# Splitting the down weights in two stages, starting the second up group with the last chunk, and three buffers for its results

## The chip, the cores and the metric

The kernel runs on one core of one Trainium2 chip. The metric is the device time of one execution in microseconds. Its engines are the tensor engine (PE, with its weight loads PEld), VectorE (DVE), ScalarE (ACT), GpSimd (POOL) and SyncE (SP), which here only issues DMAs.

## The reference, cut to what matters

One layer of a hybrid decoder over 2048 prompt rows and 64 sample rows of width 1024, in float32: a norm, a projection into eight attention heads and four mLSTM heads, both mixers, an output projection with a residual, and an MLP.

```python
def sqrelu_mlp(h, w_up, w_down):
    u = jnp.einsum('btd,df->btf', h, w_up)
    return jnp.einsum('btf,fd->btd', jnp.square(jax.nn.relu(u)), w_down)
...
h = rms_norm(x, norm2_g)
x = x + sqrelu_mlp(h, w_up, w_down)    # d_ff = 4096
y = rms_norm(x, norm_f_g)
```

The outputs also hold the sample caches of 2048 rows each, moved up by eight rows: 96 copies of 680 KB from one DRAM tensor to another, which nothing in the layer waits for.

## The kernel before, in words

**Products.** Float32 accuracy comes from splitting each operand into a rounded high part (float32r) and the low rest: ScalarE rounds (a Copy into float32r), VectorE or GpSimd subtracts, and a product is three matmuls, high × high, high × low, low × high (lines 2639 to 2641). The MLP's products are done by a seven-product scheme over 2 × 2 blocks (Winograd's form of Strassen's), so each operand also needs four sums of its blocks: seven slots instead of four.

**Stages.** `project` (line 243) works in two groups of rows, eight tiles and nine. After eight chunks of q/k for the mLSTM, each group makes five token blocks (40 + 45 tiles): the tensor engine fills one of two banks, VectorE's `tile_out` (646) rotates and copies it into a `stage` slot (two slots in group 0, three in group 1), ScalarE's `keep` (502) issues its store. GpSimd's `lo_token` (415) makes the low part of the next block's weights in two halves of 2048 columns. SyncE issues 20 of the cache copies beside group 0 (`copies`, 349). Then come `mixers`, `project_out` and `mlp` (2651).

**Up, in `mlp`.** There are 48 sets in a written order (2672): sets 0 to 15 are chunks 0 to 15 of the up weights on the first 1024 rows (512 columns a product), sets 16 to 47 the same chunks on the other rows, in two halves q of 272 columns. A set is seven chains of 12 matmuls into four banks of one of two bank sets. ScalarE's `first` (3008) copies the first chain's bank into `made[s % 2][0]`, which the fifth chain waits for; VectorE's `up_post` (3153) adds banks into three `made` buffers; ScalarE's `squares` (2980) applies relu and square and stores the four results to `K.u` in DRAM. Because the `made` buffers are two sets deep, a buffer written again waits for the store of two sets before (`u_out`). Chunk c+1's weights are loaded when set c begins, summed by VectorE (`up_sums`), rounded by ScalarE (`w_hi`) and split by VectorE (`w_low`). The operands of chunks 0 and 1 are also stored to DRAM when made (`keep`, 2800) and loaded again for sets 16 to 19 (`load_kept`, 2805); line 2839 makes SyncE wait for those stores.

**Units.** The down weights are prepared beside Up in 32 units of 256 columns: SyncE loads a quarter (`load_unit`, 2787), VectorE makes four sums (`unit_sums`, 3177), ScalarE rounds 1792 columns (`unit_hi`, 3015), VectorE splits (`unit_low`, 3187), SyncE stores both parts to `K.wd` (`store_unit`, 2793). There is one buffer, so a unit's load waits for the landed stores of the one before. They lie in sets 0 to 14, in every even set from 18 to 44, and in 27, 33 and 39 (2675). In each of these sets VectorE's queue has the sums between `up_post(s, 2)` and `up_post(s, 3)` (3249). SyncE issues one cache copy per set besides.

**Change of group.** In set 15 SyncE loads the second group's h (1088 KB a slot, five loads, 2843 to 2853) into the slots that finished chains leave. VectorE makes the sums and low parts of half q = 0, GpSimd the sums of half q = 1 (2918 to 2926), VectorE its low parts in set 16.

**Down.** 64 steps of seven chains of six matmuls (512 columns), four steps for each of 16 passes over an eighth of d_ff, with 8 short sample steps. Per step SyncE loads u (`load_u`, 2763) and a part of the next eighth of weights (`load_down`, 2822: one DMA for the high, one for the low parts), GpSimd makes u's sums (`sums`, 2928), ScalarE rounds, VectorE splits and adds into `acc` (`down_post`, 3279). GpSimd's program has `sums(0)`, `sums(1)`, then a wait for the final norm's gain (2946), then the rest. The gain's load is issued after the first step's weights (2896).

Of the kernel before, what the change touches and what calls it, by code (L numbers as in the profile page):

```python
# [6 lines left out]
F32 = mybir.dt.float32  # L7
# [6 lines left out]
P = 128  # L14
# [228 lines left out]
def project(K):  # L243
# [8 lines left out]
    with ExitStack() as ctx:  # L252
# [17 lines left out]
        wq_raw = xb[:, 1]  # L270
        xn = sb("xn", [P, 2, D])
# [31 lines left out]
        gated, dve_own, pe_state, act_state = sem("p1_gated"), sem("p1_dve_own"), sem("p1_pe_state"), sem("p1_act_state")  # L303
        tail_zero, tail_mm, tail_ev, tail_out = sem("p1_tail_zero"), sem("p1_tail_mm"), sem("p1_tail_ev"), sem("p1_tail_out")
# [20 lines left out]
        QB = (0, 16)  # L325

# [3 lines left out]
        def _(sp):  # L330
# [23 lines left out]

            for g in range(2):
                if g == 0:
                    norm.sync_group(sp, GN[0], constants)
                else:
                    for T in range(GT0[1], GT0[1] + GN[1]):
                        norm.load(sp, T, T % 2, False)  # L360
                        if T == GT0[1] + 1:
                            sp.wait_ge(lo_ready, 13)
                            load_first()
# [9 lines left out]
                for b in range(1, 5):  # L373
                    sp.wait_ge(lo_ready, b + (base + 8))
                    sp.dma_start(w_raw[:], K.w_tok[b]).then_inc(wt_in, 16)
                    if g == 0:
                        if b > 1:
                            copies(GN[0] * (b - 2) + 3, 8 if b < 4 else 4)
# [8 lines left out]
                    if b == 3:  # L387
                        tables.sync_m(sp)
                        for s in range(3):
                            sp.wait_ge(stage_out[s], 16 * (6 + (20 if s < 2 else 0)))  # L390
# [14 lines left out]
        def _(pool):  # L405
# [14 lines left out]

            qr = wq_raw.rearrange("p (k c) -> p k c", k=KC)
            for g in range(2):
# [6 lines left out]
                if g == 0:  # L429
                    lo_token(g, 1, 1)  # L430
                    with pool.Fori(1, 2) as i:
                        for j in range(2):
                            lo_token(g, 2 * i + j, j)
# [8 lines left out]
                lo_token(g, 4, 0)  # L442

        @block.scalar
        def _(act):
# [56 lines left out]
            def keep(g, b, t, slot):  # L502
                T = GT0[g] + ORDER[g][t]
                act.wait_ge(tok_ready, 40 * g + b * GN[g] + t + 1)
# [4 lines left out]
                act.dma_start(dst[T * P:(T + 1) * P, :], stage[:, slot]).then_inc(stage_out[slot], 16)  # L509

# [14 lines left out]
            for g in range(2):  # L525
                n, nn = NPC[g], GN[g]
                if g == 0:
# [4 lines left out]
                    round_chunk(0, 1, 1)  # L532
                evac(g, 0, 0, g > 0)
# [21 lines left out]
                R = 2 if g == 0 else 3  # L555
                round_block(g, 1, (qk_mm, QB[g] + n * 8))
                for t in range(nn):
                    keep(g, 0, t, t % R)
                round_block(g, 2, (tok_mm, 40 * g + nn))
                for t in range(nn):  # L560
                    keep(g, 1, t, t % R)
# [4 lines left out]
                for t in range(nn):  # L566
                    keep(g, 2, t, t % R)
# [3 lines left out]
                for t in range(nn):  # L571
                    keep(g, 3, t, t % R)
# [4 lines left out]
                for t in range(nn):  # L577
                    keep(g, 4, t, t % R)
# [23 lines left out]
        def _(dve):  # L602
# [43 lines left out]
            def tile_out(g, b, j, t, kind):  # L646
                R = 2 if g == 0 else 3
# [3006 lines left out]
```

## Time and profile before

| what | value |
|---|---|
| median of the runs | 2994.52 us (2981.97 to 2996.72, three runs) |
| profiled execution | 2992.78 us, span 2991.0 us |
| mean granted tensor clock | 0.960 of full speed |
| busy: PE, PEld, DVE, ACT, POOL | 92%, 77%, 61%, 36%, 22% of the span |
| Up (sets 0 to 47) | about 1524.7 to 2283.3 us |
| Down | 2283.3 us to the end |
| HBM | 461.65 MB read, 244.95 MB written |

The span runs from the first to the last instruction of the profiled execution; the execution's own time is 1.8 us longer. In rows of stretches each engine has its busy time and, in brackets, its instructions in the stretch; then come the granted tensor clock as a share of full speed, the mean share of time in which the 16 DMA engines moved packets, and GB/s. Lines are those of the kernel before. A helper's line stands for all who call it. Where a set begins is read from every 84th matmul of lines 2639 to 2641.

### The profile page before, as it was taken

What the parts mean: (1) busy time and instruction counts of PE and PEld (TensorE: products, weight loads), DVE (VectorE), ACT (ScalarE), POOL (GpSimd) and SP (SyncE); (2) the same over time, 40 slices, a digit from 0 to 9 for tenths busy, and PEclk for the clock granted to TensorE, in tenths of its full rate; (3) what the DMA queues carried; (4) which work ended last, traced back from release to release, by engine and by line L of the source; (5) the groups of instructions that cost most, each with busy time, mean ns of one, the idle gap of its engine ahead of it and who ended that gap; (6) DMA issues with size and microseconds to landing.
All of it is one profiled execution on the core that took longest, in us unless ns stands there. A gap on an engine that the chain in (4) does not pass through costs nothing. (4 is left out here: it accounts for less than half of the span.)

```text
span 2991.0 us, 46001 instructions
## 1 busy us (share of the span) xinstructions
PE 2737.8 (92%) x17331; PEld 2293.8 (77%) x17331; DVE 1834.0 (61%) x3890; ACT 1079.5 (36%) x1984; POOL 651.7 (22%) x539
## 2 busy tenths in 40 slices
PE   7999999999999978999879998888887999899996
PEld 5878788778777766678767886888776888778885
DVE  5522555233788755577566666555554777877776
ACT  4301322111676752423354554544443111321113
POOL 1212012120455440211100001000001344533333
PEclk9999999999999988999989998999999999999998
DMA  4464243444464548957567779576779677776762
GB/s 155 150 233 154 95 139 130 158 131 147 129 203 134 171 157 319 407 205 262 205 229 261 271 267 336 202 251 236 241 246 337 231 248 248 258 271 224 238 234 76
DMA packets 348899, 642.33 MB, mean 215 GB/s; under 512 B 39375, under 2 KB 237139, under 8 KB 328326
## 3 DMA queue, kind: packets, MB, share of 16 engines
q1 hardware_dynamic: 281516, 543.44, 52.6%
q10 hardware_dynamic: 66026, 91.95, 8.5%
q0 software_dynamic: 1152, 4.19, 0.4%
q8 instruction: 130, 2.13, 0.3%
q14 instruction: 75, 0.61, 0.1%
HBM read 461.65 MB, written 244.95 MB: 236 GB/s over the span
## 5 line engine op out<-in xcount | busy, mean ns | idle before, releaser
L2639 PE MATMUL bank<-mlp_h_hi,mlp_wu_hi 128*128 128x272 f32 (+1 forms) x1344 | 448.5, 334 | 83.5 <-ACT mlp_made L3013 47.8
L2640 PE MATMUL bank<-mlp_h_lo,mlp_wu_hi 128*128 128x272 f32 (+1 forms) x1344 | 443.6, 330 | 0.0
L2641 PE MATMUL bank<-mlp_h_hi,mlp_wu_lo 128*128 128x272 f32 (+1 forms) x1344 | 443.2, 330 | 0.0
L3293 DVE TENSOR_TENSOR mlp_acc<-mlp_acc,bank 128x512 f32<-128x512 f32 x440 | 300.2, 684 | 147.3 <-PE bank L2641 140.7
L2639 PE MATMUL bank<-mlp_wd_hi,mlp_u_hi 128*128 128x512 f32 x896 | 353.7, 395 | 36.0 <-DVE mlp_acc L3293 30.3
L2640 PE MATMUL bank<-mlp_wd_lo,mlp_u_hi 128*128 128x512 f32 x896 | 352.9, 394 | 0.0
L2641 PE MATMUL bank<-mlp_wd_hi,mlp_u_lo 128*128 128x512 f32 x896 | 352.6, 393 | 0.0
L2639 PEld LDWEIGHTS bank<-mlp_h_hi,mlp_wu_hi 128*128 128x128 f32 x1344 | 261.6, 195 | 114.5 <-issue 56.7
L3072 ACT ACTIVATE mlp_u_hi<-mlp_u_raw 128x768 fp32r<-128x768 f32 x126 | 113.0, 944 | 471.7 <-POOL mlp_u_raw L2936 471.3
L2640 PEld LDWEIGHTS bank<-mlp_h_lo,mlp_wu_hi 128*128 128x128 f32 x1344 | 261.9, 195 | 20.1
L2641 PEld LDWEIGHTS bank<-mlp_h_hi,mlp_wu_lo 128*128 128x128 f32 x1344 | 261.1, 194 | 20.0
L221 PE MATMUL p_bank<-p_w_hi,p_hT_hi 128*128 128x512 f32 x640 | 253.6, 396 | 8.7 <-DVE p_stage L671 8.7
L222 PE MATMUL p_bank<-p_w_lo,p_hT_hi 128*128 128x512 f32 x640 | 252.4, 394 | 0.0
L223 PE MATMUL p_bank<-p_w_hi,p_hT_lo 128*128 128x512 f32 x640 | 252.3, 394 | 0.0
L2639 PEld LDWEIGHTS bank<-mlp_wd_hi,mlp_u_hi 128*128 128x128 f32 x896 | 170.6, 190 | 75.9 <-DVE mlp_u_lo L3277 29.9
L2931 POOL TENSOR_TENSOR mlp_u_raw<-mlp_u_raw 128x256 f32<-128x256 f32 x64 | 58.2, 909 | 779.3 <-DMA mlp_u_raw<-u 757.4
L2641 PEld LDWEIGHTS bank<-mlp_wd_hi,mlp_u_lo 128*128 128x128 f32 x896 | 170.8, 191 | 36.0
L2640 PEld LDWEIGHTS bank<-mlp_wd_lo,mlp_u_hi 128*128 128x128 f32 x896 | 170.5, 190 | 35.3
L667 DVE TENSOR_TENSOR p_bank<-p_bank,p_rot 128x128 f32<-128x128 f32 x85 | 25.4, 298 | 273.5 <-PE p_bank L223 242.2
L1338 ACT ACTIVATE mx_probs<-mx_probs,mx_part 128x256 f32<-128x256 f32 (+1 forms) x384 | 143.4, 451 | 95.6 <-DVE mx_part L1414 95.6
L2992 ACT ACTIVATE mlp_made<-mlp_made 128x272 f32<-128x272 f32 (+1 forms) x144 | 71.0, 493 | 265.7 <-DVE mlp_made L3172 174.0
L3277 DVE TENSOR_TENSOR mlp_u_lo<-mlp_u_raw,mlp_u_hi 128x768 fp32r<-128x768 f32 x126 | 148.2, 1176 | 17.7 <-ACT mlp_u_hi L3072 17.7
(391 smaller groups left out, 5468.5 us busy)
## 6 DMA issues: line engine op xcount, KB each, us to landing
mlp_wd_lo<-wd SPq DMA_DIRECT2D x46, 1024.0 KB, 7.6
mlp_wd_hi<-wd SPq DMA_DIRECT2D x45, 1024.0 KB, 5.5
mlp_u_raw<-u SPq DMA_DIRECT2D x256, 128.0 KB, 2.3
out_win_k_sample<-in_cache_k SPq DMA_DIRECT2D x48, 680.0 KB, 7.2
out_win_v_sample<-in_cache_v SPq DMA_DIRECT2D x48, 680.0 KB, 6.4
mlp_wu_raw<-in_w_up SPq DMA_DIRECT2D x30, 1024.0 KB, 7.3
wd<-mlp_un_hi SPq DMA_DIRECT2D x32, 896.0 KB, 4.4
wd<-mlp_un_lo SPq DMA_DIRECT2D x32, 896.0 KB, 7.3
```

What stands on the lines that cost most here:

```text
L221: nc.tensor.matmul(out, ah, bh, start=(k == 0), stop=False)
L222: nc.tensor.matmul(out, ah, bl, start=False, stop=False)
L223: ins = nc.tensor.matmul(out, al, bh, start=False, stop=(k == n - 1))
L1338: ins = A(p_, p_, ACT.Exp, bias=part[a][:, n % 2, 2 * c + e, HD + 1:HW])
L2639: nc.tensor.matmul(out, ah, bh, start=fresh and k == 0, stop=False, skip_group_check=not fresh)
L2640: nc.tensor.matmul(out, ah, bl, start=False, stop=False, skip_group_check=not fresh)
L2641: ins = nc.tensor.matmul(out, al, bh, start=False, stop=k == n - 1, skip_group_check=not fresh)
L2931: g_.tensor_tensor(r[:, 3], r[:, 2], r[:, 5], ALU.add).then_inc(u_sums, 1)
L2992: ins = A(buf, src, ACT.Relu)
L3072: A(u_hi[b][:, k], u_raw[b][:, k], ACT.Copy).then_inc(u_hi_ready, 1)
L3277: v.tensor_tensor(u_lo[b][:, sl], u_raw[b][:, sl], u_hi[b][:, sl].bitcast(F32), ALU.subtract).then_inc(u_lo_ready, 1)
L3293: v.tensor_tensor(a, a, b[:], ALU.add).then_inc(summed, 1)
```

## The change

- `project`: units 0 to 10 are made beside the 40 token tiles of group 0, at tile 5 + 9w // 4, in two buffer sets by turns: SyncE loads and stores, GpSimd makes the four sums and the low part, ScalarE rounds ahead of the tile's `keep`. Group 0 has three stage slots instead of two. Its 20 cache copies leave, and sets 18 to 37 of Up issue two copies each instead of one.
- `mlp`: 21 units are left, in sets 0 to 14 and in 20, 24, ..., 40.
- The second group goes through the chunks in the order 15, 0, 1, ..., 14, so its first two sets use the operands that set 15 leaves in place. Keeping chunks 0 and 1 in DRAM goes.
- The h loads are cut in halves by q; the q = 0 halves come first.
- The second group has three `made` buffers of 272 columns, so a store has three sets.
- `K.wd` holds the high and low parts of a slot side by side, so one DMA of up to 2 MB brings both; the SBUF places of wd, acc, u, gain_f and others move. The first weights come in five pieces, the first in set 45. u of step 2 is loaded in set 47, the third and fourth acc in steps 0 and 2, acc_s and the gain in step 4.
- GpSimd's wait for the gain moves ahead of its first use.
- ScalarE's roundings of h for q = 1 stand between the squares of set 16 instead of behind them.

```diff
@@ project
+        STAGED = K.staged = (14, 13, 13)
+        UNIT_AT = {5 + 9 * w // 4: w for w in range(K.UNITS1)}
+        UNIT_LOAD = ((0, 1), (2, 3, 4), (5, 6, 7, 8), (9, 10, 11))
+            def load_unit(w):
+                e = SET[w]
+                if w < 2:
+                    sp.wait_ge(conv_out, 8)
+                    for k in range(2):
+                        sp.wait_ge(acc_out[k], 16 * 4)
+                else:
+                    sp.wait_ge(un_out[e], 32 * nth(w))
+                kb, j, c = K.unit_of(w)
+                sp.dma_start(un_raw[e][:, 0:7:2], ...).then_inc(un_in[e], 16)
+            def store_unit(w):
+                e = SET[w]
+                for hl, (src, made) in enumerate(((un_hi, un_hi_ready), (un_lo, un_lo_ready))):
+                    sp.wait_ge(made, w + 1)
+                    sp.dma_start(K.unit_rows(w, hl), src[e][:].bitcast(F32)).then_inc(un_out[e], 16)
...
                     if g == 0:
-                        if b > 1:
-                            copies(GN[0] * (b - 2) + 3, 8 if b < 4 else 4)
+                        for w in UNIT_LOAD[b - 1]:
+                            if w >= 2:
+                                store_unit(w - 2)
+                            if w < K.UNITS1:
+                                load_unit(w)
...
+                    for ev in range(36):
+                        if ev in (0, 8, 16, 24):
+                            lo_token(g, ev // 8 + 1, (ev // 8 + 1) % 2)
+                        if ev in UNIT_AT:
+                            w = UNIT_AT[ev]
+                            if w:
+                                unit_low(w - 1)
+                            unit_sums(w)
+                    unit_low(K.UNITS1 - 1)
...
+                if g == 0 and 8 * b + t in UNIT_AT:
+                    unit_hi(UNIT_AT[8 * b + t])
                 act.wait_ge(tok_ready, 40 * g + b * GN[g] + t + 1)
@@ mlp
-    UNITS = 32
+    UNITS = 32 - K.UNITS1
-    KEPT = (NC, NC + 1)
-    DOWN = (0, 2, 4, 6, 7)
+    LOADS = 2 * NC - 1
+    DOWN = (0, 4, 7, 11, 14)
+    FIRST = (0, 3, 7, 9, 11, 14)
-    sets = ... [(1, c, q) for c in range(NC) for q in range(2)]
+    sets = ... [(1, c, q) for c in (NC - 1, *range(NC - 1)) for q in range(2)]
-    unit_sets = sorted(list(range(15)) + list(range(18, 45, 2)) + [27, 33, 39])
+    unit_sets = list(range(15)) + list(range(20, 45, 4))[0:6]
+    def wait_home(eng, s, kind):
+        if 2 <= s < NC:
+            eng.wait_ge(u_out[s % 2][kind], 16 * (s // 2))
+        elif NC <= s < NC + 3:
+            for e in ((0,), (0, 1), (1,))[s - NC]:
+                eng.wait_ge(u_out[e][kind], 16 * (NC // 2))
+        elif s >= NC:
+            eng.wait_ge(v_out[(s - NC) % 3][kind], 16 * ((s - NC) // 3))
...
-                if ci <= 2:
-                    sp.wait_ge(kept_out, 32 * ci)
-                load_kept(ci + 1) if ci + 1 in KEPT else load_up(ci + 1)
-            if ci < 2:
-                keep(ci)
+                load_up(ci + 1)
...
             if s == LAST:
+                sp.wait_ge(mm, 7 * s + 1)
+                load_u(sp, 1)
+                load_first(2)
...
+                sp.wait_ge(mm, 7 * s + 5)
+                load_u(sp, 2)
             elif s != 15 and s < LAST - 1:
-                K.copy_cache(sp)
+                for e in range(2 if 18 <= s < 38 else 1):
+                    K.copy_cache(sp)
...
         def gains(F):
+            if F == 0:
+                pool.wait_ge(gain_f_in, 16)
...
         sums(0)
         sums(1)
-        pool.wait_ge(gain_f_in, 16)
```

## Rows read from the trace of the kernel before

**Rows 1.** The page, part 1: the engines.

```profile
PE 2737.8 (92%) x17331; PEld 2293.8 (77%) x17331; DVE 1834.0 (61%) x3890; ACT 1079.5 (36%) x1984; POOL 651.7 (22%) x539
```

**Rows 2.** Stretches: set 2, sets 3 to 14, then 15, 16, 17.

```profile
1568.20:1593.10 24.90, 21.31 (x85) 16.90 (x84) 13.26 (x17) 10.17 (x13) 0.00 (x0) 0.93 0.72 253
...
1593.10:1827.20 234.10, 234.10 (x1009) 189.02 (x1008) 160.97 (x209) 122.86 (x156) 0.00 (x0) 1.00 0.79 269
1827.20:1855.30 28.10, 19.71 (x86) 15.61 (x84) 13.23 (x13) 11.97 (x16) 0.00 (x0) 0.91 0.98 374
1855.30:1881.00 25.70, 16.49 (x84) 15.50 (x84) 20.77 (x14) 10.72 (x18) 12.81 (x4) 0.70 0.78 308
1881.00:1893.30 12.30, 12.16 (x84) 11.85 (x85) 8.87 (x10) 7.50 (x12) 0.00 (x0) 0.87 0.07 25
```

**Rows 3.** Stretches: sets 18-19, 20-27, 28-29, 18-47, Down's first steps.

```profile
1893.30:1914.40 21.10, 21.10 (x171) 21.10 (x169) 11.54 (x20) 10.38 (x19) 0.00 (x0) 1.00 0.62 213
1914.40:2005.90 91.50, 86.83 (x675) 84.92 (x674) 55.99 (x88) 47.14 (x89) 0.00 (x0) 1.00 0.74 257
2005.90:2043.80 37.90, 25.45 (x170) 25.04 (x170) 17.54 (x27) 13.69 (x24) 0.00 (x0) 0.82 0.65 221
1893.30:2283.30 390.00, 336.58 (x2522) 329.10 (x2520) 212.75 (x335) 180.78 (x332) 2.90 (x4) 0.95 0.73 252
2283.30:2316.10 32.80, 16.83 (x72) 13.36 (x72) 10.93 (x15) 4.46 (x7) 8.57 (x11) 0.82 1.03 384
```

**Rows 4.** Timeline in set 28: VectorE, then ScalarE.

```profile
2013.26 0.43 DVE L3182 TENSOR_TENSOR mlp_un_raw<-mlp_un_raw 128x256 f32<-128x256 f32 x1 [4.01 <-DMA mlp_un_raw<-in_w_down]
...
2015.32 0.43 ACT L2992 ACTIVATE mlp_made<-mlp_made 128x272 f32<-128x272 f32 x1 [7.65 <-DVE mlp_made L3172]
...
2018.48 0.38 ACT L3013 ACTIVATE mlp_made<-bank 128x272 f32<-128x272 f32 x1
```

**Rows 5.** Waits in sets 18 to 47: total us, times, longest.

```profile
DVE mlp_un_raw L3182 <- DMA mlp_un_raw<-in_w_down: 74.5, 17, 10.7
PE bank L2639 <- ACT mlp_made L3013: 47.8, 18, 7.1
...
ACT mlp_made L3013 <- DMA u<-mlp_made: 13.7, 9, 6.0
```

**Rows 6.** Timeline in set 16: VectorE's splits of h.

```profile
1869.20 3.26 DVE L3151 TENSOR_TENSOR mlp_h_lo<-mlp_h_raw,mlp_h_hi 128x1088 fp32r<-128x1088 f32 x1
...
1872.73 1.28 DVE L3151 TENSOR_TENSOR mlp_h_lo<-mlp_h_raw,mlp_h_hi 128x1088 fp32r<-128x1088 f32 x1
```

**Rows 7.** Waits at the start of Down.

```profile
POOL mlp_u_raw L2931 <- DMA mlp_gain_f<-in_norm_f_g: 21.9, 1, 21.9
...
PE bank L2639 <- DVE mlp_acc L3293: 16.0, 2, 14.5
```

**Rows 8.** A stretch of the projection, and three lines: duration ns min/median/max.

```profile
130.00:320.00 190.00, 186.03 (x809) 151.28 (x808) 57.65 (x176) 24.46 (x23) 36.71 (x8) 1.00 0.51 176
...
L419 POOL TENSOR_TENSOR p_w_lo<-p_w_raw,p_w_hi x16: 4539/4608/4620, 143.8 to 640.3; 128x2048 fp32r<-128x2048 f32 x16
...
L670 DVE COPY p_stage<-p_bank x85: 675/680/681, 141.8 to 729.4; 128x512 f32<-128x512 f32 x85
...
L3017 ACT ACTIVATE mlp_un_hi<-mlp_un_raw x32: 1679/1687/1691, 1551.4 to 2248.2; 128x1792 fp32r<-128x1792 f32 x32
```

**Rows 9.** DMA issues by line: KB each, median us to landing.

```profile
out_win_k_sample<-in_cache_k SPq DMA_DIRECT2D x48, 680.0 KB, 7.2
...
mlp_wu_raw<-in_w_up SPq DMA_DIRECT2D x30, 1024.0 KB, 7.3
...
wd<-mlp_un_lo SPq DMA_DIRECT2D x32, 896.0 KB, 7.3
...
u<-mlp_made ACTq DMA_DIRECT2D x128, 136.0 KB, 5.2
...
mlp_un_raw<-in_w_down SPq DMA_DIRECT2D x32, 512.0 KB, 4.7
```

More of the change, by code:

```diff
@@ L679, in _ @@
                 if g:
-                    for slot in range(2):
-                        dve.wait_ge(stage_out[slot], 16 * 20)
+                    for slot in range(3):
+                        dve.wait_ge(stage_out[slot], 16 * STAGED[slot])
                 for q, w in enumerate(GW[g]):
@@ L697, in _ @@
                 if g == 0:
-                    with chain.loop(2, 2 * n) as i:
-                        for j in range(2):
-                            for t in range(n):
-                                tile_out(g, 2 * i + j, j, t, i)
+                    for b in range(4):
+                        for t in range(n):
+                            tile_out(g, b, b % 2, t, b // 2)
                     norm.dve_scale(dve, chain, n, 0)
@@ L1745, in __init__ @@
         self.h_in = [sem(f"mlp_h_in{q}") for q in (0, 2, 4, 5)]
+        self.h_late = [sem(f"mlp_h_late{q}") for q in range(5)]
         self.h_mid, self.h_s = sem("mlp_h_mid"), sem("mlp_h_s")
@@ L3033, in _ @@
             g, c, q = sets[s]
-            ci = NC * g + c
-            early = (g == 0 or q == 1) and ci < 2 * NC - 1 and ci + 1 not in KEPT
+            ci = loaded(s)
+            early = ci + 1 < LOADS and (q == 1 if g else s < NC - 1)
             if s:
@@ L3220, in _ @@
             g, c, q = sets[s]
-            ci = NC * g + c
-            more = ci < 2 * NC - 1 and ci + 1 not in KEPT
+            ci = loaded(s)
+            more = ci + 1 < LOADS and (g == 1 or s < NC - 1)
             if s - 1 in unit_at:
@@ L3285, in down_post @@
                     dve.wait_ge(summed, steps[st.n - (4 if st.g == 0 else 5)].po0 + 7)
+            elif i == 0 and st.n == 3:
+                wait_narrow(dve, range(3))
             elif i == 2:
@@ L3433, in rows @@
                     for j in range(2):
-                        nc.tensor.matmul(out, ss[:, 2 * e + j], wd_hi[b][:, i, j], start=start and j == 0, stop=False, skip_group_check=not start)
-                        ins = nc.tensor.matmul(out, ss[:, 2 * e + j], wd_lo[b][:, i, j], start=False, stop=done and j == 1, skip_group_check=not start)
+                        nc.tensor.matmul(out, ss[:, 2 * e + j], weight(b, i, 0, j), start=start and j == 0, stop=False, skip_group_check=not start)
+                        ins = nc.tensor.matmul(out, ss[:, 2 * e + j], weight(b, i, 1, j), start=False, stop=done and j == 1, skip_group_check=not start)
                     return ins
-                for i in (0, 3, 4, 6):
+                for i in range(7):
                     weights(st, i)
```

300 lines of the change are left out of this document (170 added, 130 removed).

## The prediction

> **What bounds the kernel now.** I read the page first: the tensor engine is busy 92% of the span [rows 1], so time can only come from stretches where it waits or runs at the lower clock. The waits by engine then pointed at the MLP, and a table of stretches, cut at the starts of its 48 up sets, shows where. In the first up group (sets 0 to 15) twelve sets take 234.1 us, 19.51 each with no idle, but set 2 takes 24.9, and sets 15, 16 and 17 take 28.1, 25.7 and 12.3 [rows 2]. In the second group (sets 16 to 47, a quarter fewer columns in two halves) two undisturbed sets take 21.1 us, 10.55 each; the next eight 91.5 (11.44 each); and three times a pair takes about 38 instead of 21 with the granted clock at 0.82 [rows 3]. These pairs are 28/29, 34/35 and 40/41, each behind the extra unit in sets 27, 33 and 39, where three sets in a row make a unit.
>
> The reason is a chain of queues. In set 28 VectorE idles 4.0 us for the unit's load, its next item is the sums of that unit, and only then the addition of line 3172; ScalarE waits 7.65 us for that addition and makes the copy of line 3013, which frees the tensor engine's fifth product, at 2018.48 [rows 4]. Over the second group the tensor engine waits 47.8 us for line 3013 and VectorE 74.5 us for unit loads; 13.7 us of ScalarE's waits before that copy are for a landed store of the `made` buffer [rows 5]. At the start of Down GpSimd waits 21.9 us for the final gain, an item of no use before the last steps, with the sums of u behind it; the tensor engine loses 14.5 us [rows 7].
>
> The profiled execution took 2992.8 us, span 2991.0, 1.7 under the median of 2994.5. I make the sum against 2992.8.
>
> **Set 2, the kept up operands.** Four stores and four loads of 1.8 MB vanish, and with them the wait of line 2839 that holds SyncE's queue, behind which stand the next up load and the unit load. Set 2 goes from 24.9 to 19.5: 5.4 us. Bounds 0 and 5.4; I take 5.4, since sets 3 to 14 do the same work with units but no keeping [rows 2].
>
> **Change of group, sets 15 to 17.** Now 66.1 us [rows 2]; the floor is 19.5 + 2 × 10.55 = 40.6. The loads of h, 1088 KB each, are cut in halves, the needed ones first, and 3.7 MB of kept loads ahead of them are gone; the stretch moved 374 GB/s at a share of 0.98 [rows 2]. Halves should let the first sums start near 1841.5 instead of 1849.4, so that set 16 waits about 0.7 us instead of 8.6. What is late next is VectorE: its splits of h take 3.2 us each while GpSimd makes the other half's sums, 12.8 us in set 16, and 1.28 us when it does not [rows 2, 6]; those sums stay. Walking its queue item by item, set 16 takes 21 us (three splits at 3.2 each lie on the path), and set 17 about 17.5, since it now also carries the up operands of the next chunk (three splits of 0.7, 1.2 and 2.3 us plus four sums, kept before). Together 19.5 + 0.7 + 21 + 17.5 = 58.7, a gain of 7.4. Bounds: 0 and 20.
>
> **Second group, sets 18 to 47.** Seventeen units become six, at every fourth set. Without a unit a set costs 10.55. With one, the eight sets 20 to 27 show the price: (91.5 − 8 × 10.55)/4 = 1.8 us per unit [rows 3]. So 30 × 10.55 + 6 × 1.8 = 327.3, and 1.7 for the step into Down, 329.0, against 390.0 from 1893.3 to 2283.3: 61.0 us. Three `made` buffers instead of two let a store take another 10.5 us, which covers the landing waits; they are part of the difference, not an addition. Low bound of the gain: the three slow pairs alone, 3 × (37.9 − 22.9) = 45. High bound: 390 − 318 = 72.
>
> **The moved units.** Eleven units go into the 40 token tiles of the first projection group. There VectorE no longer does anything for them. GpSimd's split of 2048 columns takes 4.6 us [rows 8], so one of 1792 takes 4.0 and four sums of 256 about 2.3: 6.3 us per unit. A tile has 24 matmuls, 5.6 us by the 809 in 190 us [rows 8], so the units, 2.25 tiles apart, come every 12.7 us. ScalarE gets 1.69 us per unit [rows 8] ahead of a tile's store, and waits there for GpSimd. Worst is a unit behind a token split: 9.2 + 4.0 + 2.3 + 1.7 = 17.2 us. The token rounding starts about five us before the unit's tile is ready, so ScalarE is held 12 us; the third stage slot gives a store 16.8 us. I price this 0, cover: the slot; without it up to 4 places × 4 us = 16. SyncE issues 11 loads and 22 stores, 25 MB, in place of twenty 680 KB copies, 14 MB [rows 9]; the stretch has a DMA share near 0.5 [rows 8], so I price that 0 too. The loads of the next norm tiles now queue behind unit 9's stores, near 300 us, and are wanted near 319. A gain of the third slot is at most the 1.6 us that the tensor engine waits there.
>
> **The start of Down.** GpSimd's wait moves to its first gain, so sums of u go on. What is late next is u of step 2, issued in set 47 behind two weight pieces and more: 6.8 MB from 2 us into the set. At 384 GB/s, which the stretch shows at a share of 1.03 [rows 3], it lands 17.7 us later, 8 us into Down; it is wanted 11.6 us into Down. By the Trainium skill (DMA: Bandwidth & Descriptors, Specifications) one core's share of HBM is about 358 GB/s, and an estimate from that puts the landing 9.5 us into Down; the trace is already above it, so I go by the row. The 14.5 us go, with 2 us of half clock after them and 1 to 3 of other early waits. I take 15 of 18. Bounds: 5 and 20. The joined weight layout gives half as many DMAs of the same bytes: 0.
>
> **Sum.** 5.4 + 7.4 + 61.0 + 15 = 88.8. 2992.8 − 88.8 = 2904.0; against the median 2905.7. I say 2905. Its own range, from the bounds, is 2888 to 2925.
>
> **Rivals.** (a) Up operands late by DMA. The twenty copies go to sets 18 to 37, two a set. Per pair of sets SyncE and ScalarE then issue 1024 KB of weights, 8 × 136 of u, 4 × 680 of copies and half a unit, 1152: 6.1 MB in 21.1 us, 290 GB/s, where these sets moved 257 [rows 3, 9]. Against 384 that fits, and up loads stand first in SyncE's queue; but they land in 7.3 us in the median and the sums want them within 10.5. If they land at 15, each of ten pairs loses about 3 us: 2935. 15%.
>
> (b) A unit stalls even alone: the blocked addition of rows 4 recurs at each of the six, at (37.9 − 21.1)/2 = 8.4 in place of 1.8 us: 6 × 6.6 = 40 us, 2945. The undisturbed pair, whose first set has a unit, speaks against it. 8%.
>
> (c) Down's start only changes hands: step 2's u or the last weight piece arrives 10 us late, 2915. 8%; it lies inside the range.
>
> (d) Slower. The projection breaks: GpSimd's longer queue holds ScalarE's stores or VectorE's evacuation past the slots, and the tensor engine stops at each unit. It decides once a unit costs 88.8/11 = 8.1 us, for instance when VectorE's five items of a tile stand behind both GpSimd operations of 6.3 us plus a late load. Against it: VectorE's copy of a tile takes 675 to 681 ns in all 85 cases, with GpSimd splits beside some of them [rows 8], so no lock shows. The Trainium skill (SBUF — State Buffer, Who interferes with whom) says that an operation with two SBUF inputs waits for all of a GpSimd operation, and by that rule eleven units would cost 11 × 4.0 = 44 us wherever VectorE had such items; it exempts operations with one SBUF input. The tile's items read PSUM, and the trace agrees for the copy. At 12 us per unit (d) gives 2905 + 132 = 3037. 4%. (e) The change's parts cover each other and only the three slow pairs and the gain wait go: 2994.5 − 45 − 15 = 2935. 5%.
>
> The forecast keeps 60%. A measurement of this kernel tells about 0.5%, 15 us, from no change. Slower takes (d), 4%; within 0.5% needs losses of 75 us at once, 2%; faster 94%. The range for 8 in 10 must take in (a), (c) and (e) and most of the forecast's own: 2886 to 2942.
>
> **What the profile of the changed kernel would show.** Right: set 2 at 19.5 us; sets 15 to 17 in 57 to 60 us; no pair of sets in the second group above 24 us, the group at clock 1.00 after set 17, tensor waits for line 3013's successor under 10 us; no GpSimd wait for the gain near the start of Down; the stretch of rows 8 with the tensor engine busy for 186 of 190 us as now. Wrong: VectorE waiting for the up weights in sets 18 to 37 (a), a repeated gap after the six unit sets (b), tensor waits for the stage slots in the projection (d), or a gap in the second step of Down with the DMA share at 1 (c).

## The result, and the profile of the changed kernel

| | before | after |
|---|---|---|
| median of the runs | 2992.16 us (2981.97 to 2996.72, four runs) | 2881.66 us (2878.25 to 2889.47, four runs) |
| profiled execution | 2992.78 us | 2889.47 us |
| granted clock, mean | 0.960 | 0.974 |

The ratio is 0.9639, with a 95% interval of 0.9605 to 0.9672: 110.5 us less by the medians, against the 88.8 of my sum. At 2881.7 the time lies 4 us below the low end of my range (2886). The profiled execution of the changed kernel is the slowest of its four, so by the two profiles the gain is 103.3 us. The sums below are made by these.

The page, part 1 [rows 1]:

```profile
PE 2708.1 (94%) x17331; PEld 2272.2 (79%) x17331; DVE 1806.0 (63%) x3842; ACT 1086.7 (38%) x1987; POOL 726.4 (25%) x594
```

The tensor engine runs the same number of matmuls and is busy 30 us less with them, at a mean granted clock of 0.974 instead of 0.960. The rest of the 104 us of span was its idle time. The stretches, with the columns of [rows 2] and [rows 3]: set 2, sets 3 to 14, set 15, set 16, set 17, then sets 18-19, 20-27, 28-29, 18-47, and Down's first 26 us.

```profile
1564.50:1584.00 19.50, 19.50 (x86) 15.75 (x85) 13.57 (x19) 10.29 (x13) 0.00 (x0) 1.00 0.80 264
1584.00:1818.00 234.00, 234.00 (x1009) 188.98 (x1008) 159.93 (x207) 122.86 (x156) 0.00 (x0) 1.00 0.78 265
1818.00:1837.60 19.60, 19.60 (x86) 15.80 (x86) 13.98 (x13) 12.26 (x16) 0.00 (x0) 1.00 0.64 200
1837.60:1856.90 19.30, 12.91 (x85) 12.12 (x83) 16.22 (x15) 11.47 (x19) 13.48 (x4) 0.91 1.10 393
1856.90:1871.20 14.30, 11.48 (x85) 10.82 (x86) 12.67 (x16) 8.13 (x11) 0.00 (x0) 1.00 0.18 64
1871.20:1892.30 21.10, 21.10 (x170) 21.10 (x169) 11.04 (x18) 10.94 (x23) 0.00 (x0) 1.00 0.65 236
1892.30:1976.50 84.20, 84.20 (x674) 84.20 (x673) 49.16 (x79) 44.81 (x86) 0.00 (x0) 1.00 0.83 292
1976.50:1997.60 21.10, 21.10 (x170) 21.10 (x169) 14.07 (x22) 11.46 (x22) 0.00 (x0) 1.00 0.71 245
1871.20:2187.30 316.10, 316.10 (x2522) 315.88 (x2520) 178.50 (x281) 166.88 (x324) 5.61 (x8) 1.00 0.77 271
2187.60:2213.60 26.00, 23.33 (x95) 18.84 (x96) 16.07 (x21) 4.53 (x7) 5.59 (x8) 0.93 1.03 398
```

From set 18 to set 47 the tensor engine is busy 316.10 of 316.10 us at clock 1.00. There is not one gap inside this stretch, at the six units neither. Before it was 336.6 of 390.0 at 0.95. Of the MLP's sets from 2 on, only 16 and 17 still have idle time, 6.4 and 2.8 us.

Against my terms, from where the stretches begin in the two traces:

| stretch | before | after | gain | forecast |
|---|---|---|---|---|
| start to set 0 | 1524.7 | 1521.0 | 3.7 | 0 |
| set 2 | 24.9 | 19.5 | 5.4 | 5.4 |
| sets 15 to 17 | 66.1 | 53.2 | 12.9 | 7.4 |
| sets 18 to 47 and the step into Down | 390.0 | 316.4 | 73.6 | 61.0 |
| Down to the end | 707.7 | 699.2 | 8.5 | 15 |

The step into Down, the idle time between the last product of Up and the first of Down, is 1.4 us before and 0.3 after.

Waits in sets 18 to 47 that answer to [rows 5]. No wait of the tensor engine is among them:

```profile
DVE mlp_narrow L3255 <- ACT mlp_narrow L3105: 25.3, 14, 1.8
DVE mlp_un_raw L3275 <- DMA mlp_un_raw<-in_w_down: 8.0, 6, 2.2
```

VectorE waits for a unit's load 1.3 us a time instead of 4.4. At the start of Down, the waits that answer to [rows 7]:

```profile
POOL mlp_u_raw L3024 <- DMA mlp_u_raw<-u: 50.1, 4, 27.7
...
PE bank L2709 <- DMA mlp_wd<-wd: 2.6, 1, 2.6
```

GpSimd waits for u alone, no longer for the gain. The tensor engine loses 2.6 us to a load of weights instead of 14.5. The stretch of [rows 8] in the projection, and the units in it:

```profile
130.00:320.00 190.00, 186.02 (x813) 151.40 (x811) 57.67 (x177) 42.87 (x34) 113.09 (x63) 1.00 0.70 239
```

```profile
L476 POOL TENSOR_TENSOR p_un_lo<-p_un_raw,p_un_hi 128x1792 fp32r<-128x1792 f32 x11 | 44.7, 4059 | 21.1 <-ACT p_un_hi L578 21.1
L578 ACT ACTIVATE p_un_hi<-p_un_raw 128x1792 fp32r<-128x1792 f32 x11 | 18.8, 1705 | 113.6 <-POOL p_un_raw L471 87.4 <-DVE p_stage L740 26.2
```

GpSimd is busy 113 instead of 37 us of these 190, and the tensor engine 186.0, as before.

Of the signs that the prediction named as right, all came but one: sets 15 to 17 took 53.1 us, not 57 to 60.

### The profile page after: what moved, and what is told of

It is laid out like the page before. It is cut to its first block and busy times, and to the rows that moved or that the text cites. A ratio compares the mean times of both kernels' runs of the same rounds, so it can differ in the third digit from the quotient of the medians.

```text
span 2886.8 us, 45830 instructions
## 1 busy us (share of the span) xinstructions
PE 2708.1 (94%) x17331; PEld 2272.2 (79%) x17331; DVE 1806.0 (63%) x3842; ACT 1086.7 (38%) x1987; POOL 726.4 (25%) x594
## 5 line engine op out<-in xcount | busy, mean ns | idle before, releaser
L2709 PE MATMUL bank<-mlp_h_hi,mlp_wu_hi 128*128 128x272 f32 (+1 forms) x1344 | 436.2, 325 | 19.5 <-DVE mlp_h_lo L3246 13.0
L2711 PE MATMUL bank<-mlp_h_hi,mlp_wu_lo 128*128 128x272 f32 (+1 forms) x1344 | 435.3, 324 | 0.0
L2709 PE MATMUL bank<-mlp_wd,mlp_u_hi 128*128 128x512 f32 x896 | 354.2, 395 | 21.7 <-DVE mlp_acc L3388 14.4
L2710 PE MATMUL bank<-mlp_wd,mlp_u_hi 128*128 128x512 f32 x896 | 352.8, 394 | 0.0
L2711 PE MATMUL bank<-mlp_wd,mlp_u_lo 128*128 128x512 f32 x896 | 352.5, 393 | 0.0
L2709 PEld LDWEIGHTS bank<-mlp_h_hi,mlp_wu_hi 128*128 128x128 f32 x1344 | 253.9, 189 | 42.6 <-issue 16.4
L2710 PEld LDWEIGHTS bank<-mlp_h_lo,mlp_wu_hi 128*128 128x128 f32 x1344 | 253.7, 189 | 20.1
L2711 PEld LDWEIGHTS bank<-mlp_h_hi,mlp_wu_lo 128*128 128x128 f32 x1344 | 253.5, 189 | 19.8
L2709 PEld LDWEIGHTS bank<-mlp_wd,mlp_u_hi 128*128 128x128 f32 x896 | 170.6, 190 | 60.9 <-DVE mlp_u_lo L3370 15.2
L2711 PEld LDWEIGHTS bank<-mlp_wd,mlp_u_lo 128*128 128x128 f32 x896 | 170.7, 191 | 36.2
L2710 PEld LDWEIGHTS bank<-mlp_wd,mlp_u_hi 128*128 128x128 f32 x896 | 170.9, 191 | 35.7
L3235 DVE TENSOR_TENSOR mlp_wu_lo<-mlp_wu_raw,mlp_wu_hi 128x512 fp32r<-128x512 f32 (+2 forms) x93 | 127.8, 1398 | 47.5 <-ACT mlp_wu_hi L3057 47.5
```

What stands on the lines that cost most here:

```text
L2709: nc.tensor.matmul(out, ah, bh, start=fresh and k == 0, stop=False, skip_group_check=not fresh)
L2710: nc.tensor.matmul(out, ah, bl, start=False, stop=False, skip_group_check=not fresh)
L2711: ins = nc.tensor.matmul(out, al, bh, start=False, stop=k == n - 1, skip_group_check=not fresh)
L3235: v.tensor_tensor(wu_lo[ci % 2][:, k], wu_raw[ci % 2][:, k], wu_hi[ci % 2][:, k].bitcast(F32), ALU.subtract).then_inc(wu_lo_ready, 1)
```

## The experiments

Each kernel was run once beside the kernel before on the same chip. Single runs of a kernel scatter by 0.5% here, so I compare stretches of their traces. Sets 2 to 15 and the undisturbed sets of the second group repeat to 0.1 us from trace to trace, which whole times don't. Set 16 doesn't either: it took 19.4 us in some kernels and 20.4 in others whose code is the same there.

The whole times of the other eight are these. They are given for completeness; the readings below don't rest on them.

| kernel | us | the kernel before beside it |
|---|---|---|
| h_order, pool_late, down_last | 2886.57, 2895.05, 2877.25 | 2983.47 |
| b_gain | 2986.79 | 2983.47 |
| a_keep, no_units, slots2, a_gain | 2884.75, 2885.32, 2892.96, 2893.55 | 2993.77 |

### Why the second group has no gap: spacing and homes

A home is one of the `made` buffers in which a result of u waits for its store. My sum priced a unit at 1.8 us wherever it stands, and gave the wider spacing of the six that stay and the third home (`made3`) no price of their own. Four kernels take spacing and homes apart.

h2_gap4, two homes in place of three:

```diff
-        return made[s % 2][kind] if s < NC else made3[(s - NC) % 3][kind]
+        return made[s % 2][kind] if s < NC else made3[(s - NC) % 2][kind]
```

(the waits for the stores of a home likewise).

> The changed kernel with two narrow buffers per result instead of three; units still at every fourth set. Measured by the 30 sets 18 to 47, which take 316.1 us in the changed kernel. Theory S (a unit cost 1.8 us because its load was issued late, behind the stores of the unit two sets before; spacing them cured it): 316 to 318 us. Theory H (the landing waits of two-deep buffers were the cost): 6 unit sets and the sets of doubled copies lose 1 us or more each, 325 us or more. Theory V (a unit costs VectorE and ScalarE time whatever its place, 1.8 us each, my forecast): already fallen, the changed kernel pays nothing for six.

h3_gap2, the six units at every second set (20, 22, ..., 30):

```diff
-    unit_sets = list(range(15)) + list(range(20, 45, 4))[0:6]
+    unit_sets = list(range(15)) + list(range(20, 31, 2))
```

> The changed kernel with its six units at sets 20, 22, ..., 30, two apart as before, three buffers kept. Theory S: the units after the first are late again, about 1 us or more each in sets 22 to 31: 321 to 327 us for sets 18 to 47. Theory H: the third buffer hides it, 316 to 318 us.

h2_gap2, both edits.

> Two buffers and units two sets apart: the regime of the kernel before inside the changed one. Both theories: about 1.8 us a unit, 325 to 330 us for sets 18 to 47. If it stays at 316, neither is the cause and the rest of the traffic of the kernel before (17 units) is.

h3_burst, three homes, units in sets 22, 23, 24 and 30, 31, 32:

> Three buffers, units in two bursts of three, sets 22, 23, 24 and 30, 31, 32, as 26, 27, 28 were before. Theory S for the slow pairs (one unit buffer: store, landing, load, landing take about 19 us, more than a set of 10.5): each burst costs 12 to 17 us in the set of its last unit and the next, at half clock for part of it, 340 to 350 us for sets 18 to 47. Theory H: under 325 us.

They took 2903.65, 2916.55, 2917.03 and 2926.52 us, with the kernel before at 2995.37. Sets 18 to 47 of each, in this order (one line from each trace):

```profile
1870.20:2204.70 334.50, 321.42 (x2522) 319.61 (x2520) 178.58 (x282) 166.02 (x323) 5.88 (x8) 0.99 0.72 256
```

```profile
1876.20:2217.70 341.50, 324.03 (x2521) 321.80 (x2520) 177.38 (x281) 165.70 (x324) 5.83 (x8) 0.98 0.71 251
```

```profile
1874.50:2216.60 342.10, 324.50 (x2522) 322.39 (x2520) 178.09 (x281) 165.85 (x323) 5.63 (x8) 0.98 0.71 251
```

```profile
1874.40:2226.70 352.30, 325.88 (x2523) 324.91 (x2521) 177.66 (x282) 167.06 (x324) 6.13 (x8) 0.96 0.69 242
```

| sets 18 to 47, us | units every 2nd set | every 4th set |
|---|---|---|
| two homes | 342.1 | 334.5 |
| three homes | 341.5 | 316.1 (the change) |

At close spacing the third home is worth 0.6 us and with two homes the wide spacing is worth 7.6, but the two together are worth 26.0. Each removes one of two waits, and either wait is enough to stop the tensor engine. All four kernels issue two cache copies a set in sets 18 to 37, so the table holds for this traffic. The waits of h2_gap4 in these sets:

```profile
ACT mlp_narrow L3105 <- DMA u<-mlp_narrow: 32.5, 12, 4.0
...
PE bank L2709 <- ACT mlp_narrow L3105: 13.1, 6, 2.8
...
DVE mlp_un_raw L3275 <- DMA mlp_un_raw<-in_w_down: 4.9, 4, 2.3
```

With two homes, ScalarE's first copy of a set (line 3105) waits for a store of u of two sets earlier. The unit load is hardly waited for. In h3_gap2 it is the reverse:

```profile
DVE mlp_un_raw L3275 <- DMA mlp_un_raw<-in_w_down: 37.6, 6, 8.0
...
PE bank L2709 <- ACT mlp_narrow L3105: 16.4, 5, 4.3
```

SyncE's queue shows why the load is late there. The up load and the unit load of set 22, first in h3_gap2:

```profile
1918.52 0.63 SPq L2880 DMA_DIRECT2D mlp_wu_raw<-in_w_up  x1
1922.27 0.62 SPq L2886 DMA_DIRECT2D mlp_un_raw<-in_w_down  x1
```

and in the changed kernel, set 24:

```profile
1934.62 0.63 SPq L2880 DMA_DIRECT2D mlp_wu_raw<-in_w_up  x1
1935.29 0.63 SPq L2886 DMA_DIRECT2D mlp_un_raw<-in_w_down  x1
```

At close spacing the unit load is issued 3.75 us behind the up load, since SyncE first waits for the previous unit's stores. At wide spacing it follows 0.67 us behind, with nothing to wait for. Landing takes 9.7 us in the median against 7.2. The theory of the late load (S) holds for spacing and falls for homes, where it had expected at most 2 us of loss and 18.4 came. The theory of the landing waits (H) holds for homes. The sizes of S were too low in all four kernels. The burst cost 36.2 us, all in four sets, two of which I read for the clock below.

In h2_gap4 the stall comes two sets behind a unit, in sets 22, 26, 30, 34 and 38 (2.4 to 4.6 us each), and not behind the sixth unit, in set 40: set 42 takes 10.5. In the sets right behind the first five units the last stores of u landed after 10.0 to 10.8 us; behind the sixth, where one copy a set is issued instead of two, after 8.3. So the doubled copies look like a part of this wait. No kernel without them was run, and their share stays open.

The way from the kernel before to the changed one can be split at h2_gap2. The kernel before lost 72.5 us over the floor of 316.1 (sets 18 to 47 without the step into Down), h2_gap2 loses 26.0. So 46.5 us went with the rest of the change, above all with eleven units fewer and no three units in a row, and 26.0 with spacing and home together. That both losses come to 4.3 us per unit is chance. In the kernel before, the three slow pairs hold 50.5 of the 72.5 us, and the other 14 units cost 22.0, 1.6 each; h2_gap2 has no such pairs, and its units, at the same spacing but beside two copies a set, cost 4.3 each.

### The change of group

h_order, the halves of each slot of h loaded together again in the order of the slots:

```diff
                 M.load_h(sp, K, 0, 0, 1, M.h_in[0], 0)
+                M.load_h(sp, K, 0, 0, 1, M.h_late[0], 1)
                 sp.wait_ge(mm, 7 * s + 2)
                 M.load_h(sp, K, 1, 1, 1, M.h_in[1], 0)
+                M.load_h(sp, K, 1, 1, 1, M.h_late[1], 1)
...
-                M.load_h(sp, K, 0, 0, 1, M.h_late[0], 1)
-                M.load_h(sp, K, 1, 1, 1, M.h_late[1], 1)
```

> The changed kernel with the two halves of each h slot loaded together again in the order of the slots, instead of first halves first. Theory H (my forecast was 5.6 us too high at the change of group because the first halves, 0.56 MB a slot, are all in by 1830 in the changed kernel and VectorE's sums and splits of them run there free of GpSimd): VectorE's sums of h begin about 5 us later, more of its splits lie beside GpSimd's sums and take over 2 us, sets 15 to 17 take 57 to 61 us instead of 53.1. Theory T (set 15 with its own chain times is what hides them, whatever the order): 52.5 to 54 us.

Sets 15, 16 and 17 of h_order:

```profile
1814.90:1835.20 20.30, 19.68 (x85) 15.57 (x84) 13.24 (x13) 12.19 (x16) 0.00 (x0) 1.00 0.82 279
1835.20:1859.00 23.80, 15.25 (x84) 14.40 (x84) 20.77 (x15) 10.60 (x17) 12.83 (x4) 0.78 0.79 271
1859.00:1873.90 14.90, 13.93 (x85) 13.42 (x86) 12.77 (x16) 9.35 (x13) 0.00 (x0) 0.77 0.06 21
```

Together 59.0 us, 5.8 more than the changed kernel's 53.2 (4.8 more than in the kernels whose set 16 took 20.4), as theory H has it. Only 0.9 us of the 5.8 is more idle time of the tensor engine. The rest is its busy time for the same products, 48.9 instead of 44.0 us, at a granted clock of 0.78 and 0.77 in sets 16 and 17 instead of 0.91 and 1.00. Its longest stand in these sets is 5.0 us in h_order, for the first of the splits below, and 2.1 us in the changed kernel. So the order of the loads is worth little in waiting and much in clock. VectorE's splits in set 16, in h_order and then in the changed kernel:

```profile
1838.23 7.13 DVE L3246 TENSOR_TENSOR mlp_h_lo<-mlp_h_raw,mlp_h_hi 128x1088 fp32r<-128x1088 f32 x2
...
1845.63 3.26 DVE L3246 TENSOR_TENSOR mlp_h_lo<-mlp_h_raw,mlp_h_hi 128x1088 fp32r<-128x1088 f32 x1
...
1849.15 3.26 DVE L3246 TENSOR_TENSOR mlp_h_lo<-mlp_h_raw,mlp_h_hi 128x1088 fp32r<-128x1088 f32 x1
...
1852.68 1.28 DVE L3246 TENSOR_TENSOR mlp_h_lo<-mlp_h_raw,mlp_h_hi 128x1088 fp32r<-128x1088 f32 x1
```

```profile
1839.96 2.50 DVE L3246 TENSOR_TENSOR mlp_h_lo<-mlp_h_raw,mlp_h_hi 128x1088 fp32r<-128x1088 f32 x2
...
1843.88 2.10 DVE L3246 TENSOR_TENSOR mlp_h_lo<-mlp_h_raw,mlp_h_hi 128x1088 fp32r<-128x1088 f32 x1
...
1846.53 3.01 DVE L3246 TENSOR_TENSOR mlp_h_lo<-mlp_h_raw,mlp_h_hi 128x1088 fp32r<-128x1088 f32 x1
...
1849.80 3.26 DVE L3246 TENSOR_TENSOR mlp_h_lo<-mlp_h_raw,mlp_h_hi 128x1088 fp32r<-128x1088 f32 x1
```

Five splits take 14.9 us in the one and 10.9 in the other. The order of the loads gives VectorE its sums 2 us earlier (12.4 instead of 14.5 us into set 15), while GpSimd starts at nearly the same place (23.7 instead of 23.3 us into set 15). So the first two of these five splits run before it instead of beside it, and the third overlaps it only in part.

pool_late carries this to the end: GpSimd's sums of the second half wait for all seven splits of the first.

```diff
+        pool.wait_ge(h_lo_ready, 14)
         pool.wait_ge(M.h_s, 8)
```

> The changed kernel with GpSimd's four sums of the second half of h held back until VectorE has made all seven low parts of the first half. Theory P (VectorE and GpSimd slow each other: alone a split takes 1.25 us, beside a GpSimd sum 2.1 to 3.3): the splits of set 16 that took 2.10, 3.01 and 3.26 take about 1.3 each, set 16 is 3 to 4 us shorter than 19.4; the second half's sums start at about 1848 and set 17 gives part of it back: sets 16 and 17 together 30 to 33 us against 33.6. Theory N (the long splits come from something else, DMA writes for instance): they stay over 2 us and sets 16 and 17 get longer by the later sums, over 36 us.

Its splits take 1.28 us each, and a sum of GpSimd 2.48 us. The third line is a sum of GpSimd in the changed kernel, beside the splits, 3.46 us:

```profile
1848.06 1.28 DVE L3247 TENSOR_TENSOR mlp_h_lo<-mlp_h_raw,mlp_h_hi 128x1088 fp32r<-128x1088 f32 x1
```

```profile
1855.95 2.48 POOL L3015 TENSOR_TENSOR mlp_h_raw<-mlp_h_raw 128x1088 f32<-128x1088 f32 x1
```

```profile
1848.46 3.46 POOL L3016 TENSOR_TENSOR mlp_h_raw<-mlp_h_raw 128x1088 f32<-128x1088 f32 x1
```

The mechanism (P) is shown, but not the gain: sets 16 and 17 take 37.8 us instead of 33.6. GpSimd starts 11.9 us into set 16 instead of 4.2, and ahead of set 17's first product the tensor engine stands 8.9 us for the splits that wait for these sums:

```profile
PE bank L2709 <- DVE mlp_h_lo L3247: 10.1, 2, 8.9
```

Side by side is the better bargain here: 3.53 us for a pair of operations that take 3.76 in turn.

### The start of Down

b_gain, the kernel before with one wait moved; a_gain, the changed kernel with it moved back (and the gain's load at step 0 again). The edit of b_gain:

```diff
         sums(1)
-        pool.wait_ge(gain_f_in, 16)
...
         def gains(F):
+            if F == 0:
+                pool.wait_ge(gain_f_in, 16)
```

> The kernel before with one edit: GpSimd waits for the gain of the final norm at the first use of it, not ahead of the loop of Down's steps. Theory G (my forecast's term: the gain wait is what holds the start of Down, 15 of 18 us): the PE gap of 14.87 us at 2301 falls to at most 3 and Down, from its first product to the end, is 12 to 15 us shorter than 709. Theory U (two waits in a row: the gain landed 2310.1, but the operands of pair 2 were only asked for at 2293.4, after the first steps, and would have landed at about 2302): GpSimd starts the third sums at about 2302 to 2303 instead of 2310.1, the gap falls to 7 to 9 us, and 6 to 8 us are won; the rest of the changed kernel's 14 comes from its asking for pair 2 during the last up set.

> The changed kernel with GpSimd's wait for the final gain ahead of the loop of Down's steps again, and the gain loaded at Down's first step, as before the change; pair 2 stays loaded in the last up set. Moving the wait alone in the kernel before won 8.4 us at Down's start. Theory W (the wait costs what it holds back): the gain lands at 2207 to 2210, GpSimd's third sums start then instead of 2202.1, and the third step of Down, which could start about 2212, waits 2 to 5 us. Theory S (it costs as much here as there): 7 to 9 us. Theory 0 (the earlier load of pair 2 hides it): under 1 us.

In b_gain the third sums start when their own operands land:

```profile
2302.80 0.72 POOL L2931 TENSOR_TENSOR mlp_u_raw<-mlp_u_raw 128x256 f32<-128x256 f32 x1 [15.34 <-DMA mlp_u_raw<-u]
```

That is 2302.8 instead of 2310.1. The gap in the tensor engine falls from 14.5 to 7.7 us. Behind it the clock is low for less time (granted 0.83 instead of 0.60 from 2300 to 2320 us), and Down runs 8.4 us earlier from there on. By its last products 6.3 of them are left, and the whole time of this run, 2986.79 beside 2983.47 us, shows no gain; a gain of this size is within the scatter. Theory U holds: two waits stood one behind the other, and the gain was the later. The changed kernel also asks earlier for u of step 2 ("pair 2" in the expectations). It gets 14.2 us counted from Down's first product and 1.1 ahead of it. In a_gain the gain lands at 2210.8:

```profile
2210.88 0.72 POOL L3025 TENSOR_TENSOR mlp_u_raw<-mlp_u_raw 128x256 f32<-128x256 f32 x1 [23.71 <-DMA mlp_gain_f<-in_norm_f_g]
```

```profile
PE bank L2709 <- DVE mlp_acc L3388: 8.3, 1, 8.3
```

and Down is 11.4 us later from there. That is more than any of the three theories had. W, with 2 to 5 us, took the landing about right; that it took the chain behind it (sums, rounding, splits, then the clock) too short is my reading and not shown. The wait costs 8.4 us before the change and 11.4 after it.

### Down's sample steps

Of the 14.2 us won at its start, Down had 8.3 left at its last products. 4.2 of the loss are gaps ahead of the eight sample steps, 4.4 us against 0.2 before (start to start, over the shortest step from one product to the next). The trace has these waits:

```profile
PE bank L3526 <- DVE mlp_acc L3388: 1.9, 2, 1.0
PE bank L3526 <- DMA mlp_wd<-wd: 1.4, 2, 1.1
```

The new layout makes the last of an eighth's loads 1.5 MB instead of 1.0 MB, and a sample step waits for all four. down_last cuts them otherwise:

```diff
-    DOWN = (0, 4, 7, 11, 14)
+    DOWN = (0, 4, 7, 12, 14)
```

> The changed kernel with the four loads of a down eighth's operands cut 2.0, 1.5, 2.5 and 1.0 MB instead of 2.0, 1.5, 2.0 and 1.5 (the last one as small as before the change). Between the first Down product and the last, the changed kernel lost about 5.9 us again on the kernel before, after having won 14.2 at the start; its sample steps wait up to 1.5 us, in two places for the weights' load. Theory L (the last, larger load lands after the sample step that reads all four wants to start): the gaps ahead of the sample steps fall to under 0.6 us, Down ends 4 to 6 us earlier against its own start, 695 instead of 699.8 us in all. Theory C (the waits come from the copies of eighth boundaries and the earlier start, not from the cut): the gaps stay, Down stays within 1 us of 699.8. If the third load, now 2.5 MB, becomes the late one, pair 1 or 2 of an eighth shows new gaps of about 1 us and the gain is under 2.

From Down's first product to the last it took 672.2 us instead of 677.8, as theory L has it. But nine other kernels with the uncut layout, run for other purposes, took 672.2 to 676.1 (a_gain aside), and their gaps ahead of sample steps came to 0.4 to 2.8 us, with 2.1 in down_last. So the profiled execution of the changed kernel was the worst of its kind in this stretch, and the cut shows no effect beyond that scatter. In the two traces of the old layout these gaps are 0.2 and 0.0, so the layout does seem to cost something, 0.4 to 2.8 us in those nine. By which of its loads stays open. Its whole time, 2877.25 us, is no evidence either: Up began at 1514.7 in that run, in code that is the same in all.

### Kept operands, units, and the slot

a_keep, the kept operands of two chunks stored again and waited for:

```diff
+                if s <= 2:
+                    sp.wait_ge(kept_out, 32 * s)
                 load_up(ci + 1)
+            if s < 2:
+                keep(ci)
```

> The changed kernel with the rounded parts of the first two chunks of the up weights stored to memory again, and SyncE waiting for these stores ahead of the next loads, as before the change (nobody reads them). Theory K (my forecast's term: the stores of the kept operands were the whole stall of set 2): set 2 takes 24 to 26 us again instead of 19.51, 5 to 6 us more in all. Theory B (in the changed kernel the bandwidth freed elsewhere hides them, and the term was never theirs): set 2 stays at 19.5 to 21.

```profile
1559.50:1584.50 25.00, 21.17 (x85) 16.75 (x84) 13.26 (x17) 10.17 (x13) 0.00 (x0) 0.93 0.72 251
```

Set 2 takes 25.0 instead of 19.5 us. The 5.4 us were all due to these stores and the wait for them; the two were not taken apart.

no_units, without the eleven units in the projection (the stretch from 120 to 320 us; GpSimd 39 instead of 114 us):

```diff
-        UNIT_AT = {5 + 9 * w // 4: w for w in range(K.UNITS1)}
+        UNIT_AT = {}
```

> The changed kernel without the eleven units of the down weights in the projection: neither loaded, rounded nor stored there. Down reads the fourth eighth's operands in place of the first three's, so the output leaves these weights out; its time is that of the same number of products and bytes. Theory Z (my forecast's price of 0 for the moved units): the last product of the projection starts at 724 to 729 us, as in the other runs of the changed kernel and in the kernel before (725.2, 728.5). Theory M (they cost something that the other parts hide): it starts 5 to 16 us earlier, 710 to 720.

```profile
120.00:320.00 200.00, 197.47 (x857) 160.27 (x855) 64.44 (x179) 31.63 (x32) 39.34 (x9) 1.00 0.28 100
```

The last product of the projection starts at 730.0. With the units and three slots it starts at 721.6 to 730.9 in eleven traces, and before the change at 728.5. A stretch between fixed instructions says it more closely: from VectorE's first to its fortieth copy into a stage slot, the 40 tiles of group 0, it takes 199.4 us in no_units and 197.5 to 199.3 with the units. The units cost nothing that shows.

slots2, two stage slots in the first half of the projection (the counts of their uses likewise):

```diff
-            return t % 3 if g else (8 * b + t) % 3
+            return t % 3 if g else t % 2
```

> The changed kernel with two stage slots instead of three in the first half of the projection. Theory C (the third slot is the cover that lets the units ride free: ScalarE works 49 us instead of 30 and GpSimd 114 instead of 39 in the stretch from 120 to 320 us): TensorE waits for stage slots, the last product of the projection starts 6 to 20 us later than 725, and the longest waits are for the stage or the low parts of the weights. Theory F (the stretch has so much slack on ScalarE and GpSimd that two slots do): it starts at 724 to 730 as before.

```profile
PE p_bank L221 <- DVE p_stage L740: 6.6, 3, 4.8
```

One stretch of it, between the same matmuls 85.9 us long in the changed kernel (215.7 to 301.6), is 92.9 us here, and the projection's last product starts at 734.1. So the cover is real and worth 7 us. Of these, the waits for a stage slot make 5.0 (6.6 against 1.6 us in the projection up to 430 us); behind the longest, of 4.8 us, the granted clock is at 0.50 for 3.4 us.

## Why the forecast came out as it did

The direction and the places were right, and so was the second group as by far the largest term. The total came out 22 us too small against the medians, and 15.4 too small against the spans of the two profiles. Of the latter, the second group gave 12.6 us more than forecast, the change of group 5.5 more, the time ahead of Up 3.7 more, and Down 6.5 less.

**The price of a unit, the step that failed.** I took 1.8 us per unit from sets 20 to 27 of before [rows 3] and charged it to the six that stay, 10.8 us. It is zero at every fourth set with three homes, 3.1 in the mean with two homes (18.4/6) and 4.3 at every second set with two homes. A price read where units stand close was carried to a spacing at which its cause, SyncE's wait for the previous unit's stores, no longer exists. The rows had said so: sets 18 and 19 hold a unit with none close before it, and take 21.1 us, the floor. I used them against rival (b) and not for the price. The division by four also leaves out the unit of set 27; with it the price is 1.4 us, and 8.5 us of the fault remain. The other 1.8 of the 12.6 us is mostly the step into Down, 0.3 us instead of 1.7. The sentence that the third buffer was "part of the difference, not an addition" failed too: without it 18.4 of the 73.6 us would be missing. My bound of 72 took the step at 1.7 us, and lies below the 73.6 that came.

**The change of group.** This is the second term that came out too small: sets 15 to 17 at 58.7 forecast, 53.2 measured. I walked VectorE's queue with three long splits on the path. The diff puts all the first halves ahead of the late ones; I had said that the needed halves come first and hadn't asked which splits would then still meet GpSimd's sums. With the loads in slot order the sum is 59.0, close to the forecast by luck: the three sets take 20.3, 23.8 and 14.9 us there, and 19.5, 21.7 and 17.5 in my walk. Set 17 was the larger part of the miss, 17.5 forecast and 14.3 measured, and the order explains 0.6 of its 3.2 us. For the rest no kernel was run, and the cause stays open.

**Set 2** was exact, and a_keep shows the cause. **The moved units**, priced 0, cost nothing that shows, though GpSimd works 7.0 us on each (4.06 for the low part, four sums of 0.74) and not 6.3. The cover that I named holds: without the slot 7 us are lost, within my bound of 16. The 3.7 us by which Up begins earlier are scatter; over the eleven traces of kernels with three slots and the changed MLP, Up begins at 1514.7 to 1524.9, and in the two of before at 1523.7 and 1524.7.

**The start of Down** came out right in size, 15 forecast, 14.2 and 1.1 measured. But the ground was half wrong, and so luck had a part: the gain wait alone is worth 8.4, and the earlier request for u of step 2, which I had treated as what is late next, supplies the rest. That u landed 14.4 us into Down, not 8, and by my own reading it was wanted at 11.6; yet the tensor engine stood only 2.6 us there, for weights. What the term left out is the later loss, 5.9 us in the profiled execution and 0.8 to 5.0, 2.0 in the median, in nine other kernels; the sample steps are a part of it. The difference, some 4 us, is a part of what separates the 103 us of the profiles from the 110 of the medians; for the rest there is no trace of the faster executions.

**The rivals.** (a) fell: the stretch moves 271 GB/s, VectorE waits for the up weights' load four times there, 4.3 us in all, and the tensor engine for none of it. (b) fell, and h2_gap4 shows what kept it away: the blocked copy comes back with two homes, behind five of the six units. (c) is the 2.6 us wait for weights. (d) fell with no_units: no lock shows on the copies, which take 681 to 683 ns in all 85 cases beside GpSimd's units too. (e) fell in all parts.

## What to carry to other kernels

A price per event that is read where events stand close holds only at that spacing: before carrying it to another one, name the wait it consists of and ask whether it is still there. Look for the row in which the event stands alone. Two changes that each remove one of two parallel waits have no prices of their own, and only the two-by-two table shows it (0.6 and 7.6 us apart, 26.0 together). A sum that comes out near the forecast proves nothing as long as its parts don't. Compare stretches between fixed instructions rather than whole times when the runs of one kernel scatter by 0.5%.

## What the runs showed of the hardware

VectorE's split of 128x1088 and GpSimd's sum of the same size take 1.28 and 2.48 us alone, and 3.26 and 3.46 us side by side, at one of each per 3.53 us. The Trainium skill (SBUF — State Buffer, Who interferes with whom) describes the shared port as an exclusive lock held for a whole instruction. One after the other would be 3.76 us, so the trace nearly agrees with it.

A store of 136 KB of u, 1.7 us at the least, lands after 7.5 us in the median and 13.2 at the most in the second group of the changed kernel. In h2_gap4, with a home reused every 21 us instead of every 31, landings of 10.0 to 10.8 us right behind a unit went with a stop of the tensor engine, and one of 8.3 us did not.

In h3_burst the tensor engine stood for 7.1 us in set 24 and 6.4 in set 25, and the granted clock in the two was 0.83 and 0.82 of full speed, where it had been at its higher level before:

```profile
1937.60:1957.20 19.60, 12.47 (x87) 12.28 (x86) 7.85 (x11) 6.23 (x13) 0.00 (x0) 0.83 0.78 278
1957.20:1976.70 19.50, 13.10 (x85) 12.88 (x85) 9.70 (x16) 7.57 (x12) 0.00 (x0) 0.82 0.64 226
1976.70:1997.80 21.10, 21.10 (x171) 21.10 (x170) 11.17 (x18) 11.26 (x24) 0.00 (x0) 1.00 0.91 330
```

The gaps in h2_gap4 were of 2.1 to 2.8 us, one behind each of five units, and one of 0.5. Behind those of 2.7 and 2.8 us in sets 30 and 34 the clock fell for 3.4 us, behind the one of 2.8 us in set 22 it didn't. The stretch behind the gap in set 30:

```profile
2012.50:2015.90 3.40, 3.40 (x17) 3.40 (x16) 0.99 (x3) 1.64 (x4) 0.00 (x0) 0.50 1.31 538
```

Set 22, without the fall, took 3.1 us more than 10.55 with a gap of 2.8; set 30, with it, 4.5 more with a gap of 2.7; set 24 of h3_burst 9.0 more with a gap of 7.1. What a gap costs beyond its length is thus mostly the fall of the clock behind it, and short gaps are not spared it: in both kernels the loss over the floor is 1.4 times the idle time (18.4 for 13.1 us, 36.2 for 26.4).
